# Attention of a two-layer encoder step: keys cast in parts, maxima ahead of the copies of sums, a row cleared by GpSimd

## The chip, the cores and the metric

The kernel runs on one core of a Trainium2 chip. The metric is the device time of one execution in microseconds; the median of three runs is 2562.42 us (2562.3 to 2562.77). All numbers of the trace are of one further, profiled execution.

## The reference

One inference step of two layers, over 16 learned meta tokens, a prompt of 1024 tokens and a running stream of 32 tokens with 128 past ones. Cut to what matters here:

```python
z = rmsnorm(x) @ w_in                      # query rank 768, latent 256, rotary key 32, two RG-LRU inputs of 512
q = (rmsnorm(c_q) @ w_uq)                  # 8 heads of 64 + 32 (rotary) columns
kv = ckv_keys @ w_ukv                      # per head: 64 key and 64 value columns
s = (q_nope . k_nope + q_pe . k_pe) * SM_SCALE      # rotary key k_pe is shared by all heads
s = where(key_chunk <= query_chunk, s, -1e30)
o = softmax(s) @ v
h = x + concat(rmsnorm(o), rmsnorm(y_lru)) @ w_out
h = h + square(relu(rmsnorm(h) @ w_up)) @ w_down
```

The output must hold the accuracy of float32, so the kernel splits each operand of a product into a high part (float32r) and a low part (the difference) and multiplies high by high, high by low and low by high.

## The kernel before, in words

Each engine has its own program, written out by hand; nothing schedules it but the order of the code and the waits on semaphores. `w(name, k)` waits until the semaphore `name` has come to `k` in this layer. Per layer come the input projections, the attention, the output projection, and an MLP which takes the greater part of the time. The change touches the attention alone.

The keys stand in 1296 columns (meta tokens, prompt, stream, past), the queries in 1074. Heads go in turn through two slots: even heads use `qe`, `keh`, `kel`, odd heads `qo`, `koh`, `kol` (queries, keys high, keys low). In each slot some partitions hold the head's own 64 key or query rows, others the 32 rotary rows, and one row holds the shift, which takes the maximum of each query's scores off. In the odd slot the shift row is row 32, inside the rows that the maxima's product reads (all 128), so it must be zero while maxima are made.

Before the loop over heads TensorE makes the four key products (L743, read by ScalarE into `kf`) and the ten value products (L918), with the maxima steps of head 0 among them. Then the loop goes over 8 heads and 19 pairs of a query bank and a key tile (`NP = 19`). For each pair TensorE (L946) multiplies the exponentials of three pairs ago with the values, and (L961) makes the scores of the new pair. At pairs 2 to 12 it also does one of the eleven maxima steps of the **next** head (L893, `MAXES`), on the high parts only. VectorE reduces each step from PSUM (`reduce_max`, L1986). The two PSUM banks of the maxima take turns: step s waits until the reduction of step s-2 is done. At pair 13 VectorE folds the parts together (`all_parts`, L1993), at pair 14 TensorE transposes the result (L899), ScalarE and VectorE make the shift of it (L1371, L1997), and DMAs of SyncE and GpSimd (L2502, L2503) put it into the shift row, which the next head's first scores wait for.

At the start of head h's loop VectorE loads the slot of head h+1: the rotary queries (`load_q`, L1959; for odd heads from 3 on it first clears the shift row, L1957) and the keys' high part (`load_k`, L1972). ScalarE casts the other query rows (L1350). GpSimd then makes the low parts (`low_parts`, L2476): three subtractions, two for the queries and one for the keys, after it has waited for all three high parts. The rotary keys are the same for all heads and are written once for each slot: for the odd slot VectorE casts them in the loop of head 0 (`kslot_hi`, L1976) and subtracts them to a low part at pair 4 (`kslot_lo`, L1690). The casts of head 1's keys wait for the last value product, because `koh` and `kol` lie where that product reads `ckvl`.

When a query bank is finished (pair 2, 8 or 18, seen four pairs later: at pairs 6, 12, and 3 of the next head) VectorE copies the row of sums out of PSUM (`sums_out`, L2009) and ScalarE the output. In the loops of heads 2, 4 and 6 VectorE also inverts the sums of two heads, at pair 10 (L2013).

## Time and profile before

| | |
|---|---|
| median of three runs | 2562.42 us |
| profiled execution | 2563.18 us, its span 2561.3 us |
| mean granted TensorE clock | 0.997 |
| TensorE busy | 2537.1 us (99%) |
| VectorE busy | 1767.7 us (69%) |
| ScalarE busy | 1029.1 us (40%) |
| GpSimd busy | 287.9 us (11%) |
| TensorE's share of the chain that ended last | 96% |
| of it the scores L961, values L946, maxima L893 | 4%, 5%, 2% |

PE is TensorE's matmuls, PEld its weight loads, DVE VectorE, ACT ScalarE, POOL GpSimd, SP SyncE. In a timeline a row is one instruction or several alike behind one another, with its start from the span's start, its length, and in brackets the engine's idle time in front of it and what ended that ("issue": nothing that the profile shows). Ends of matmuls are modelled, so two matmuls' lengths can overlap; their starts are the better measure. The first layer's loop over heads begins at 307 us, the second layer's at 1579 us, and a head takes some 20 us.

### The profile page before, as it was taken

The page shows a single profiled execution, that of the slowest core. Times are in us where ns is not written, and L with a number is a line of the kernel's source. Part 1 is how long each engine was busy: PE and PEld are TensorE (multiplying, and loading weights), DVE is VectorE, ACT ScalarE, POOL GpSimd, SP SyncE. Part 2 cuts the span into 40 slices and gives each one's busy share as a digit, 9 for nine tenths or more (in the row PEclk, how much of TensorE's full clock was granted, in tenths as well). Part 3 has the DMA queues.
Part 4 walks back from the last instruction along what each step waited for, and adds up shares of the span by engine and source line. Part 5 has one row for each costly group of instructions (what it writes and reads, how often), then busy time and mean ns, then how long its engine had stood idle before and what let it go on. Part 6 is the DMA issues. An engine that isn't in the chain of part 4 may idle for free.

```text
span 2561.3 us, 43462 instructions
## 1 busy us (share of the span) xinstructions
PE 2537.1 (99%) x18088; PEld 2452.9 (96%) x18088; DVE 1767.7 (69%) x2554; ACT 1029.1 (40%) x1777; POOL 287.9 (11%) x206
## 2 busy tenths in 40 slices
PE   9999999999999999999999999999999999999997
PEld 9999877999999999999999998779999999999997
DVE  8679766598666665666776796665985656666666
ACT  5464355445232322323424644553443323232325
POOL 0123344100000000000001233441000000000002
PEclk9999999999999999999999999999999999999998
DMA  4121201211121111112221121012111111121112
GB/s 157 50 65 63 59 10 40 92 57 50 34 63 38 55 46 43 58 34 67 83 81 58 58 70 51 11 45 94 50 50 50 50 42 59 34 67 34 63 38 77
DMA packets 54704, 143.86 MB, mean 56 GB/s; under 512 B 9280, under 2 KB 12448, under 8 KB 54512
## 3 DMA queue, kind: packets, MB, share of 16 engines
q1 hardware_dynamic: 49600, 129.62, 15.5%
q0 software_dynamic: 4768, 11.45, 1.4%
q8 instruction: 145, 2.38, 0.4%
q14 instruction: 47, 0.39, 0.1%
q10 hardware_dynamic: 144, 0.04, 0.0%
HBM read 127.37 MB, written 11.36 MB: 54 GB/s over the span
## 4 chain that ended last, share of the span: by engine, by line
PE 96%; DVE 2%; issue 1%; ACT 1%; DMA 1%; POOL 0%; SPq 0%; ACTq 0%; DVEq 0%; POOLq 0%
PE ps L1096 29%; PE ps L743 26%; PE ps L1067 24%; PE ps L946 5%; PE ps L961 4%; PE ps L1015 2%; PE ps L893 2%; PE ps L810 1%; PE ps L918 1%; PE ps L1093 0%; PE ps L772 0%; DMA qe<-mt 0%; PE ps L831 0%; DVE mxp L1986 0%; DVE msq L2367 0%
## 5 line engine op out<-in xcount | busy, mean ns | idle before, releaser
L2275 DVE TENSOR_TENSOR xall<-xall,ps 128x536 f32<-128x536 f32 (+1 forms) x504 | 355.6, 706 | 202.8 <-PE ps L1096 202.7
L1096 PE MATMUL ps<-fh,whi 128*128 128x268 f32 (+1 forms) x2016 | 412.4, 286 | 0.0
L1096 PE MATMUL ps<-fh,wlo 128*128 128x268 f32 (+1 forms) x2016 | 412.4, 286 | 0.0
L1096 PE MATMUL ps<-fl,whi 128*128 128x268 f32 (+1 forms) x2016 | 412.3, 286 | 0.0
L1473 ACT ACTIVATE whi<-raw 128x512 fp32r<-128x512 f32 x218 | 136.5, 628 | 561.5 <-PE ps L1096 556.4
L1096 PEld LDWEIGHTS ps<-fh,whi 128*128 128x128 f32 x2016 | 314.7, 189 | 0.3 <-issue 0.2
L1096 PEld LDWEIGHTS ps<-fl,whi 128*128 128x128 f32 x2016 | 314.1, 189 | 0.0
L1096 PEld LDWEIGHTS ps<-fh,wlo 128*128 128x128 f32 x2016 | 314.0, 189 | 0.0
L2129 DVE TENSOR_TENSOR wlo<-raw,whi 128x512 fp32r<-128x512 f32 x218 | 150.5, 692 | 195.6 <-ACT whi L1473 193.9
L1986 DVE TENSOR_REDUCE mxp<-ps 64x1 f32<-64x64 f32 (+11 forms) x384 | 140.9, 372 | 53.8 <-PE ps L893 46.9
L1145 ACT ACTIVATE whi<-raw 128x1024 fp32r<-128x1024 f32 (+3 forms) x72 | 66.7, 926 | 233.6 <-PE ps L743 231.2
L743 PE MATMUL ps<-xgh,whi 128*128 128x358 f32 (+1 forms) x720 | 157.3, 327 | 0.0
L743 PE MATMUL ps<-xgl,whi 128*128 128x358 f32 (+1 forms) x720 | 156.6, 325 | 0.0
L743 PE MATMUL ps<-xgh,wlo 128*128 128x358 f32 (+1 forms) x720 | 156.5, 325 | 0.0
L1504 ACT ACTIVATE ff<-ps 128x536 f32<-128x536 f32 (+1 forms) x96 | 59.1, 616 | 188.6 <-PE ps L1067 173.0
L743 PEld LDWEIGHTS ps<-xgl,whi 128*128 128x128 f32 x720 | 124.0, 189 | 0.0
L743 PEld LDWEIGHTS ps<-xgh,whi 128*128 128x128 f32 x720 | 123.3, 189 | 0.5 <-issue 0.2
L743 PEld LDWEIGHTS ps<-xgh,wlo 128*128 128x128 f32 x720 | 123.3, 189 | 0.0
L1662 DVE TENSOR_TENSOR wlo<-raw,whi 128x1024 fp32r<-128x1024 f32 (+3 forms) x70 | 87.3, 1247 | 40.0 <-ACT whi L1145 39.6
L1510 ACT ACTIVATE ff<-ff 128x536 f32<-128x536 f32 (+1 forms) x128 | 83.2, 650 | 76.9 <-DVE ff L2233 75.3
L2218 DVE TENSOR_TENSOR ff<-ff,ps 128x536 f32<-128x536 f32 (+1 forms) x90 | 63.8, 708 | 67.8 <-PE ps L1067 67.8
L1473 ACT ACTIVATE whi<-draw 128x512 fp32r<-128x512 f32 x128 | 80.8, 632 | 73.0 <-PE ps L1067 73.0
(556 smaller groups left out, 5836.6 us busy)
## 6 DMA issues: line engine op xcount, KB each, us to landing
raw<-in_wst SPq DMA_DIRECT2D x140, 512.0 KB, 3.7
draw<-in_wst SPq DMA_DIRECT2D x128, 256.0 KB, 2.7
xall<-in_xT SPq DMA_DIRECT2D x16, 537.0 KB, 7.4
x_scratch<-xall POOLq DMA_DIRECT2D x8, 537.0 KB, 3.4
xall<-x_scratch SPq DMA_DIRECT2D x8, 537.0 KB, 5.6
rc<-sum_scratch POOLq DMA_DIRECT2D x16, 268.0 KB, 4.1
ra<-qr SPq DMA_DIRECT2D x16, 134.2 KB, 2.4
out_ckv_out<-ckv POOLq DMA_DIRECT2D x4, 536.0 KB, 4.3
```

The source lines that it names most:

```text
L743: mm = nc.tensor.matmul(dst(q), wt, r(q), start=(k == 0 and i == 0), stop=(k == n - 1 and i == 2))
L946: mm = nc.tensor.matmul(ps[0:65, bank, c0:c0 + n], v[:, v0:v0 + 65], p_tile(gk)[:, 0:n], start=(k in FIRST), stop=(k in LAST))
L961: mm = nc.tensor.matmul(ps[:, gi % 3, 0:n], ks[e][0 if a == "h" else 1][rows, k0:k0 + P], qs[e][0 if c == "h" else 1][rows, q0:q0 + n], st ...
L1067: mm = nc.tensor.matmul(ps[:, 2 * slot_ + q, 0:HN], wt, rhs[:, q * HN:(q + 1) * HN], start=(opens and kk == 0 and i == 0), stop=(kk == 3 a ...
L1096: mm = nc.tensor.matmul(ps[:, 2 * s + q, 0:HN], wt, rhs[:, q * HN:(q + 1) * HN], start=(kk == 0 and i == 0), stop=(kk == 1 and i == 2))
L1145: nc.scalar.activation(whi[b % 2][:, 0:n], raw[b % 2][:, 0:n], ACT.Copy).then_inc(S["w_hi"], 1)
L1473: nc.scalar.activation(ring(pairs("u_hi", j) + u, whi), src, ACT.Copy).then_inc(S["u_hi"], 1)
L1510: nc.scalar.activation(ff[c][:, 0:N2], ff[c][:, 0:N2], ACT.Square).then_inc(S["f_sq"], 1)
L1662: V.tensor_tensor(wlo[b % 2][:, 0:n], raw[b % 2][:, 0:n], whi[b % 2][:, 0:n].bitcast(F32), ALU.subtract).then_inc(S["w_lo"], 1)
L1986: ins = V.reduce_max(mxp[lo_:hi_, tile, part:part + 1], ps[lo_:hi_, max_bank(h, s), c0:c0 + n], AX_X)
L2129: V.tensor_tensor(ring(spot, wlo), src, ring(spot, whi).bitcast(F32), ALU.subtract).then_inc(S["u_lo"], 1)
L2275: V.tensor_tensor(xq, xq, pair_slot(DOWN_SLOT[n % 3], L), ALU.add).then_inc(S["d_add"], 1)
```

## The change

Four edits, all in the attention.

1. **Head 1's keys in two parts.** Instead of two casts of 1296 columns (the head's keys, the rotary keys), VectorE makes both for the columns 0 to 400 and then both for the rest (`load_second`). TensorE's first three maxima steps of head 1 wait for the first parts alone, the fourth (`K_STEPS = 3`) for all.
2. **The low rotary keys in three places.** `kslot_lo` of the odd slot is cut in three pieces of 432 columns: the first right behind the casts and ahead of all reductions, the others behind the reductions at pairs 3 and 4.
3. **Maxima ahead of copies.** In each pair `reduce_max` and `all_parts` now come before `sums_out`.
4. **GpSimd clears the shift row** of heads 3, 5 and 7 (`clear_shift`), as its first step for such a head, when the scores that used the slot are done; TensorE's first maxima step of these heads waits for it. GpSimd's `low_parts` waits for the keys only ahead of its third subtraction, for every head.

```diff
+K_FIRST, K_STEPS = 400, 3
+K_PARTS = [(0, 432), (432, 864), (864, KW)]
...
@@ TensorE, max_step @@
-                        w("k_hi", h + 1)
+                        if h != 1:
+                            w("k_hi", h + 1)
...
+                        if e == 1 and h >= 3:
+                            pe.wait_ge(S["slot1_set"], L * PER["slot1_set"] + 2 + h // 2)
...
+                    if h == 1 and s == K_STEPS:
+                        w("k_hi", 2)
+                        w("kslot_hi", 3)
...
@@ VectorE @@
-                    if h % 2 == 1 and h >= 3:
-
-                        V.memset(qs[1][0][32:33, :].bitcast(F32), 0.0)
...
-                def kslot_hi(e):
-
-                    V.tensor_copy(ks[e][0][KEY_ROWS[e], :], kpe[KEY_ROWS[e], :]).then_inc(S["kslot_hi"], 1)
+
+                def load_second():
+
+                    w("mm", U_V + 10)
+                    dst, src, rows = slot_parts(1)[2]
+                    V.tensor_copy(dst[0][rows, 0:K_FIRST], src[rows, 0:K_FIRST])
+                    V.tensor_copy(ks[1][0][KEY_ROWS[1], 0:K_FIRST], kpe[KEY_ROWS[1], 0:K_FIRST]).then_inc(S["kslot_hi"], 1)
+                    V.tensor_copy(dst[0][rows, K_FIRST:KW], src[rows, K_FIRST:KW]).then_inc(S["k_hi"], 1)
+                    V.tensor_copy(ks[1][0][KEY_ROWS[1], K_FIRST:KW], kpe[KEY_ROWS[1], K_FIRST:KW]).then_inc(S["kslot_hi"], 1)
...
-                def kslot_lo(e):
-
-                    w("kslot_hi", e + 1)
-                    lo(ks[e][1][KEY_ROWS[e], :], kpe[KEY_ROWS[e], :], ks[e][0][KEY_ROWS[e], :], "kslot_lo")
+                def kslot_lo(e, a, b):
+
+                    w("kslot_hi", 3 if e else 1)
+                    lo(ks[e][1][KEY_ROWS[e], a:b], kpe[KEY_ROWS[e], a:b], ks[e][0][KEY_ROWS[e], a:b], "kslot_lo")
...
                         if i == 0 and h + 1 < NH:
                             if h:
                                 load_q(h + 1)
-                            load_k(h + 1)
-                            if h == 0:
-                                kslot_hi(1)
+                                load_k(h + 1)
+                            else:
+                                load_second()
+                                kslot_lo(1, *K_PARTS[0])
                         if h == 0 and i == 15:
                             split(30)
+                        if h + 1 < NH:
+                            if i in MX_AT:
+                                reduce_max(h + 1, MX_AT.index(i))
+                            if h == 0 and i in (3, 4):
+                                kslot_lo(1, *K_PARTS[i - 2])
+                            if i == MX_END:
+                                all_parts(h + 1)
+                                shift_lo(h + 1)
                         for n_bank in range(3):
                             hb, ib = divmod(h * NP + i - OUT_LAG - BANK_LAST[n_bank], NP)
                             if ib == 0 and hb >= 0:
                                 sums_out(hb, n_bank)
-                        if h + 1 < NH:
-                            if i in MX_AT:
-                                reduce_max(h + 1, MX_AT.index(i))
-                            if h == 0 and i == 4:
-                                kslot_lo(1)
-                            if i == MX_END:
-                                all_parts(h + 1)
-                                shift_lo(h + 1)
...
@@ GpSimd @@
+                def clear_shift(h):
+
+                    pool.wait_ge(S["s"], L * PER["s"] + (h - 1) * NP)
+                    pool.wait_ge(S["q_lo"], L * PER["q_lo"] + h)
+                    G.memset(qs[1][0][32:33, :].bitcast(F32), 0.0).then_inc(S["slot1_set"], 1)
+                    pool.wait_ge(S["slot1_set"], L * PER["slot1_set"] + 2 + h // 2)
+
                 def low_parts(h):
 
+                    if h % 2 == 1 and h >= 3:
+                        clear_shift(h)
                     w("qn_hi", h + 1)
                     w("q_hi", h + 1)
-                    w("k_hi", h + 1)
-                    for dst, src, rows in slot_parts(h):
+                    for n, (dst, src, rows) in enumerate(slot_parts(h)):
+                        if n == 2:
+                            w("k_hi", h + 1)
                         ins = G.tensor_tensor(dst[1][rows, :], src[rows, :], dst[0][rows, :].bitcast(F32), ALU.subtract)
                     ins.then_inc(S["q_lo"], 1)
```

Three places of the instruction order show what moves. The new file's lines are numbered some ten to twenty higher; a row has the line, the operation, its operands and size, and what it waits for. The first place is VectorE at the start of head 0's loop, first layer (`koh`, `kol`: the odd slot's keys; `kpe`: the rotary keys). Before:

```order
L1972 CAST koh_136<-kf0_123 64x1296 [waits mm]
L1976 CAST koh_136<-kpe_86 64x1296
L1986 TENSOR_REDUCE mxp<-ps 128x1 [waits mxmm]
L1986 TENSOR_REDUCE mxp<-ps 64x1
L1986 TENSOR_REDUCE mxp<-ps 128x1
L1986 TENSOR_REDUCE mxp<-ps 64x1
L1986 TENSOR_REDUCE mxp<-ps 16x1
L1986 TENSOR_REDUCE mxp<-ps 128x1 [waits mxmm]
L1986 TENSOR_REDUCE mxp<-ps 64x1
L1986 TENSOR_REDUCE mxp<-ps 128x1 [waits mxmm]
L1690 TENSOR_TENSOR kol_137<-kpe_86,koh_136 64x1296 [waits kslot_hi]
```

Now:

```order
L1984 CAST koh_136<-kf0_123 64x400 [waits mm]
L1985 CAST koh_136<-kpe_86 64x400
L1986 CAST koh_136<-kf0_123 64x896
L1987 CAST koh_136<-kpe_86 64x896
L1700 TENSOR_TENSOR kol_137<-kpe_86,koh_136 64x432 [waits kslot_hi]
L1997 TENSOR_REDUCE mxp<-ps 128x1 [waits mxmm]
L1997 TENSOR_REDUCE mxp<-ps 64x1
L1997 TENSOR_REDUCE mxp<-ps 128x1
L1997 TENSOR_REDUCE mxp<-ps 64x1
L1997 TENSOR_REDUCE mxp<-ps 16x1
L1997 TENSOR_REDUCE mxp<-ps 128x1 [waits mxmm]
L1997 TENSOR_REDUCE mxp<-ps 64x1
```

The low part of the rotary keys stood behind the third step's reduction; now its first third stands ahead of the first one, behind four casts, and the other two behind the second and third step's.

The second place is GpSimd's program from head 1's low parts on, first layer (`qo` and `qe` are the slots' queries, `mt` the shift). Before:

```order
L2476 TENSOR_TENSOR qo_133<-qn0_116,qo_133 64x1074 [waits k_hi,q_hi,qn_hi]
L2476 TENSOR_TENSOR qo_133<-ra0_127,qo_133 32x1074
L2476 TENSOR_TENSOR kol_137<-kf0_123,koh_136 64x1296
L2502 DMA qo_133<-mt_257 1x2x16 [waits mt_lo]
L2503 DMA qo_133<-mt_257 1x2x32
L2476 TENSOR_TENSOR qe_132<-qn1_117,qe_132 64x1074 [waits k_hi,q_hi,qn_hi]
L2476 TENSOR_TENSOR qe_132<-ra1_128,qe_132 32x1074
L2476 TENSOR_TENSOR kel_135<-kf1_124,keh_134 64x1296
L2502 DMA qe_132<-mt_257 1x2x16 [waits mt_lo]
L2503 DMA qe_132<-mt_257 1x2x32
L2476 TENSOR_TENSOR qo_133<-qn1_117,qo_133 64x1074 [waits k_hi,q_hi,qn_hi]
L2476 TENSOR_TENSOR qo_133<-ra1_128,qo_133 32x1074
```

Now:

```order
L2499 TENSOR_TENSOR qo_133<-qn0_116,qo_133 64x1074 [waits q_hi,qn_hi]
L2499 TENSOR_TENSOR qo_133<-ra0_127,qo_133 32x1074
L2499 TENSOR_TENSOR kol_137<-kf0_123,koh_136 64x1296 [waits k_hi]
L2525 DMA qo_133<-mt_257 1x2x16 [waits mt_lo]
L2526 DMA qo_133<-mt_257 1x2x32
L2499 TENSOR_TENSOR qe_132<-qn1_117,qe_132 64x1074 [waits q_hi,qn_hi]
L2499 TENSOR_TENSOR qe_132<-ra1_128,qe_132 32x1074
L2499 TENSOR_TENSOR kel_135<-kf1_124,keh_134 64x1296 [waits k_hi]
L2525 DMA qe_132<-mt_257 1x2x16 [waits mt_lo]
L2526 DMA qe_132<-mt_257 1x2x32
L2487 MEMSET qo_133 1x1074 [waits q_lo,s]
L2499 TENSOR_TENSOR qo_133<-qn1_117,qo_133 64x1074 [waits q_hi,qn_hi,slot1_set]
```

The wait `k_hi` has moved from the first to the third subtraction of every head, and one memset stands ahead of head 3's.

The third place is VectorE at pairs 10 to 14 of head 1's loop, first layer (`srow`: the row of sums; `mx`: the folded maxima). Before:

```order
L1986 TENSOR_REDUCE mxp<-ps 128x1 [waits mxmm] x3
L1986 TENSOR_REDUCE mxp<-ps 64x1 x2
L1986 TENSOR_REDUCE mxp<-ps 128x1 [waits mxmm]
L2009 COPY srow_147<-ps 1x384 [waits pv]
L1986 TENSOR_REDUCE mxp<-ps 128x1 [waits mxmm]
L1986 TENSOR_REDUCE mxp<-ps 64x1
L1993 TENSOR_REDUCE mx<-mxp 128x10 [waits mxt,mxred]
```

Now:

```order
L1997 TENSOR_REDUCE mxp<-ps 128x1 [waits mxmm] x3
L1997 TENSOR_REDUCE mxp<-ps 64x1 x2
L1997 TENSOR_REDUCE mxp<-ps 128x1 [waits mxmm] x2
L1997 TENSOR_REDUCE mxp<-ps 64x1
L2020 COPY srow_147<-ps 1x384 [waits pv]
L2004 TENSOR_REDUCE mx<-mxp 128x10 [waits mxt,mxred]
```

The copy of the sums has moved from ahead of the eleventh step's two reductions to behind them, directly ahead of the folding reduction.

## Rows read from the trace of the kernel before

**Rows 1.** Timeline of TensorE, loop of head 0 (columns: start, length, engine, line, operands)
```profile
309.34 0.48 PE L893 MATMUL ps<-koh,qo 128*128 128x144 f32 x3 [0.94 <-DVE koh L1976]
...
311.95 0.34 PE L893 MATMUL ps<-koh,qo 128*128 128x400 f32 x1
...
315.94 0.51 PE L893 MATMUL ps<-koh,qo 128*128 128x144 f32 x2 [0.53 <-DVE mxp L1986]
...
1587.51 0.50 PE L893 MATMUL ps<-koh,qo 128*128 128x144 f32 x2 [0.52 <-DVE mxp L1986]
```

**Rows 2.** Timeline of VectorE, loops of heads 0 and 1, first layer
```profile
307.18 0.83 DVE L1972 CAST koh<-kf 64x1296 fp32r<-64x1296 f32 x1 [3.09 <-PE ps L918]
...
308.04 0.83 DVE L1976 CAST koh<-kpe 64x1296 fp32r<-64x1296 f32 x1
...
309.86 2.08 DVE L1986 TENSOR_REDUCE mxp<-ps 128x1 f32<-128x80 f32 x7 [0.99 <-PE ps L893]
...
312.83 2.32 DVE L1690 TENSOR_TENSOR kol<-kpe,koh 64x1296 fp32r<-64x1296 f32 x1
...
330.22 1.28 DVE L1986 TENSOR_REDUCE mxp<-ps 128x1 f32<-128x80 f32 x5 [1.27 <-PE ps L893]
```

**Rows 3.** Timeline of GpSimd, loop of head 0, first layer
```profile
304.06 0.51 POOL L2503 DMA_DIRECT2D qe<-mt  x1
...
308.18 3.04 POOL L2476 TENSOR_TENSOR qo<-qn,qo 64x1074 fp32r<-64x1074 f32 x1 [3.61 <-DVE koh L1972]
...
313.84 4.11 POOL L2476 TENSOR_TENSOR kol<-kf,koh 64x1296 fp32r<-64x1296 f32 x1
```

**Rows 4.** Timelines of GpSimd and VectorE where the rotary keys are made
```profile
209.28 3.11 POOL L2436 TENSOR_TENSOR sqa<-sqa,sqa 128x1074 f32<-128x1074 f32 x1 [1.27 <-ACT sqa L1277]
...
210.47 2.49 DVE L1865 COPY kpe<-kpe 32x1074 f32<-32x1074 f32 x1
```

**Rows 5.** Timelines of VectorE and TensorE, opening of head 2's loop
```profile
347.00 0.95 DVE L1957 MEMSET qo<- 1x1074 f32 x1 [2.69 <-PE ps L961]
...
347.97 0.71 DVE L1959 CAST qo<-ra 32x1074 fp32r<-32x1074 f32 x1
...
349.75 0.49 PE L893 MATMUL ps<-koh,qo 128*128 128x144 f32 x3 [0.30 <-issue]
```

**Rows 6.** Timelines around the keys of head 0 (last row: second layer)
```profile
281.48 0.83 DVE L1972 CAST keh<-kf 64x1296 fp32r<-64x1296 f32 x1 [0.69 <-ACT kf L1362]
...
282.48 2.50 POOL L2476 TENSOR_TENSOR qe<-qn,qe 64x1074 fp32r<-64x1074 f32 x1 [1.28 <-DVE keh L1972]
...
283.20 0.70 PE L893 MATMUL ps<-keh,qe 96*128 96x144 f32 x4
...
1553.88 2.49 POOL L2476 TENSOR_TENSOR qe<-qn,qe 64x1074 fp32r<-64x1074 f32 x1 [0.85 <-DVE keh L1972]
```

**Rows 7.** Timelines of TensorE and VectorE, pairs 12 to 14 of head 1's loop
```profile
341.37 0.41 PE L893 MATMUL ps<-keh,qe 96*128 96x512 f32 x1
...
341.44 0.56 DVE L2009 COPY srow<-ps 1x384 f32<-1x384 f32 x1
...
342.93 0.20 DVE L1993 TENSOR_REDUCE mx<-mxp 128x10 f32<-128x40 f32 x1
...
343.21 0.29 PE L899 MATMUL ps<-ident,mx 128*128 128x128 f32 x1
```

**Rows 8.** The same place in head 2's loop
```profile
361.29 0.69 DVE L1986 TENSOR_REDUCE mxp<-ps 128x1 f32<-128x512 f32 x1
...
361.44 0.42 PE L893 MATMUL ps<-koh,qo 128*128 128x512 f32 x1
```

**Rows 9.** GpSimd clearing rows, L2493 (min/median/max ns, first and last start)
```profile
L2493 POOL MEMSET qo<- x4: 987/988/989, 291.1 to 1563.5; 32x1074 f32 x4
```

**Rows 10.** TensorE's waits; windows: us, busy of the engines, granted clock, DMA share
```profile
PE ps L997 <- POOL msq L2542: 4.8, 1, 4.8
...
2550.00:2555.00 5.00, 2.04 (x4) 1.17 (x4) 3.73 (x10) 2.17 (x3) 0.00 (x0) 0.50 0.93 339
```

More of the change, by code:

```diff
@@ L472, in trunk @@
             ("y_sq", 4), ("y_sum", 3), ("y_n", 4), ("v_one", 1), ("v_ev", 10), ("kf", 4),
-            ("kslot_hi", 2), ("kslot_lo", 2),
-            ("slot1_set", 2), ("p_zero", 5), ("qn_hi", NH), ("q_hi", NH), ("k_hi", NH), ("q_lo", NH), ("s", NH * NP), ("p", NH * NP),
+            ("kslot_hi", 3), ("kslot_lo", 4),
+            ("slot1_set", 2 + NH // 2 - 1), ("p_zero", 5), ("qn_hi", NH), ("q_hi", NH), ("k_hi", NH), ("q_lo", NH), ("s", NH * NP), ("p", NH * NP),
             ("pv", NH * NP), ("mxmm", NH * NMX), ("mxred", NH * NMX), ("mxc", NH), ("mxt", NH), ("mt_hi", NH), ("mt_lo", NH),
@@ L956, in _ @@
                             if h == 1:
-                                w("kslot_lo", 2)
+                                w("kslot_lo", 4)
                         if gi >= 3:
@@ L1964, in load_k @@
                         w("kf", 1)
-                    if h == 1:
-                        w("mm", U_V + 10)
                     if h == 2:
@@ L2005, in sums_out @@
                     if h == 0 and n == 0:
-                        w("kslot_lo", 2)
+                        w("kslot_lo", 4)
                     r = slice(64 * (h % 2), 64 * (h % 2) + 1)
@@ L2031, in _ @@
                     if s == 3:
-                        kslot_lo(0)
+                        kslot_lo(0, 0, KW)
                     if s == 7:
```

## The prediction

> **What bounds the kernel now.** I read the waits of TensorE first. In this stage they are short, and a stage in which TensorE hardly waits can gain only what those waits are. Then I read the first head of the attention loop, engine by engine, since the change rewrites its opening. Here s0 to s10 are the eleven steps that compute a head's maxima (L893), r0 to r10 VectorE's reductions of them (L1986), and "head 1" is the second head, whose maxima are made while head 0's scores run.
>
> TensorE waits at s0 of head 1 for the rotary half of the keys, 0.94 us, and at s5 for r3, 0.53 us [rows 1]. VectorE explains both. It casts the two halves of the keys (0.83 us each), then reduces, and subtracts the low rotary part (L1690) in one piece of 2.32 us in front of r3 [rows 2]. That piece ought to be shorter: GpSimd was at work beside it [rows 3]. So the third view is GpSimd's, and the question is what happens when both read SBUF.
>
> The trace answers it. A GpSimd operation ran from 209.28 to 212.39; a VectorE copy of 32x1074, started at 210.47, took 2.49 us, where the cast of that shape takes 0.71 [rows 4, 5]. It ended 0.57 us behind GpSimd's end: it had stood still. It goes the other way too: GpSimd's qo operation at 308.18 took 3.04 us against 2.50 for its like [rows 3, 6], since the cast begun at 308.04 held it up. And they take turns: VectorE's 2.32 us subtraction began at 312.83, was held until GpSimd's operation ended (just before 313.84) and needed 1.37 more; GpSimd's next one, from 313.84, then took 4.11 us. **One waits for the whole instruction of the other.**
>
> The Trainium skill says the same more widely (SBUF — State Buffer, "SBUF: two separate sides"): the port pair of VectorE and GpSimd is an exclusive lock, and a VectorE operation in a 2-port mode or with two SBUF inputs, and a GpSimd operation, block each other for an instruction's length. The trace agrees for the 2.49 us copy; that a cast is held up in the same way no row here shows alone. By this rule the change is slower, and the rule is my forecast's mechanism; without it the sum would be the second rival's.
>
> **The change part by part.**
>
> *GpSimd no longer waits for the keys before a head's two query subtractions.* For head 1 both queries are ready long before, so they start behind the shift DMAs, at 304.06 + 0.51 = 304.57 [rows 3], 3.6 us earlier than now. At 2.50 us each [rows 6] they hold GpSimd until about 307.15 and 309.7 (at 2.1 us each, a bound from 3.04 less the cast's part of it, until 308.9). VectorE's first key cast starts at 307.18 [rows 2]: it falls into the second one, or slips in and its successor waits. Call the moment at which GpSimd's second operation ends U; I take 309.5 (308.9 to 309.9).
>
> *The keys of head 1 in two parts.* From 0.83 us at 1296 columns and 0.71 at 1074 [rows 2, 5] a column costs 0.54 ns and an instruction 0.13 us: 0.35 us for 400 columns, 0.61 for 896. The first cast, held up, ends 0.2 behind U, the second at U + 0.58. TensorE started s0 0.47 us after the last cast's end now (308.04 + 0.83 to 309.34), so s0 comes at U + 1.05 = 310.55, against 309.34: 1.2 us late, where a free port would have made it 0.9 early.
>
> *The rest of the keys and the first third of the low part, ahead of r0.* The two 896-column casts end at U + 1.22 and U + 1.86. The first of them releases GpSimd's kol operation, which asks while the second runs, and is next: about 2.8 us (4.11 less the 1.3 that it was held up) until U + 4.7. The low piece of 432 columns asks in the meantime and waits; it ends at U + 5.15 (a third of 1.37). Only then r0, 1.28 us (the five pieces at 330.22), until U + 6.46 = 315.95. s2 needs r0: it starts at 316.0 against 311.95. TensorE would have come to it at 310.55 + 2.61 = 313.15, so it waits 2.85 us in one piece. From s2 to s5 TensorE needs 3.99 us with the wait of 0.53 in it [rows 1], 3.46 without; the two later thirds (0.5 us each, GpSimd done) fit between r1, r2 and r3. s5 comes at 319.45 against 315.94: **3.5 us per layer, 7.0 in both**; the second layer has the same wait at s5 (1587.51). With U from 308.9 to 309.9 it is 2.9 to 3.9 per layer.
>
> *The same in head 0.* GpSimd was free from 282.48 - 1.28 = 281.20 and stood for the keys' cast [rows 6]. Now it starts at once, and the cast, ready at 281.48, waits until 281.26 + 2.50 = 283.76 and ends at 284.45. TensorE's s0, at 283.20 now with no wait, comes at about 284.55: 1.3 us (0.9 to 1.5). In the second layer the cast ended at about 1553.88 - 0.17 = 1553.71 (GpSimd followed it by 0.17 in the first: 281.48 + 0.83 = 282.31 to 282.48), so it had begun at about 1552.85, before GpSimd came free (1553.88 - 0.85 = 1553.03): it keeps the port, and this costs nothing.
>
> *Maxima ahead of copies of sums.* At pairs 3 and 6 VectorE swaps two operations that it runs back to back; nobody waits for either. At pair 12 the copy moves from in front of r10 to behind it, in front of the reduction (L1993) that the transpose waits for. VectorE ends r9 just before 341.44, TensorE s10 only at 341.37 + 0.41 = 341.78 [rows 7]. Now the copy fills that pause. After the change VectorE stands until 341.82 and does r10 and the copy, which take 342.93 - 341.44 = 1.49 us together: L1993 starts at 343.31, 0.38 later. The transpose (343.21) follows L1993's end (343.13) within 0.08 and would wait 0.30 to 0.38; I take 0.35. In heads 2, 4 and 6 the reciprocal has pushed r9 to 361.29, s10 ends at 361.86 before r9 does, and the order is free [rows 8]. Left are the loops of heads 0, 1, 3 and 5 in two layers: 8 x 0.35 = **2.8 us**. The DMAs behind the transpose move with TensorE, and give nothing back.
>
> *GpSimd clears the odd heads' shift row.* VectorE's memset of 0.95 us goes (347.00), and TensorE waits 0.30 us at s0 there (349.75) [rows 5, 9]. GpSimd's memset takes 0.99 for 32 rows of that width; the trace shows none of one row, and I take the same. It asks when VectorE casts the query: cast 0.71, memset, then the key cast of 0.83, ends at about 349.35 against 349.54 now. If the port is not shared for a memset, the gain is all of 0.30; if GpSimd is late, it is nothing. I take 0.2 in five of six places: -1.0 (0 to -1.8). The new wait in front of s0 is met by 348.7. Behind it GpSimd's query subtractions wait, which are needed some 15 us later.
>
> **Sum:** 7.0 + 1.3 + 2.8 - 1.0 = +10.1 us on the profiled execution's 2563.18, so 2573.3; that execution lies 0.76 over the median of 2562.42, which gives **2572.5**.
>
> **The rivals.**
> - *Only the casts are held up.* If the low piece gets the port before GpSimd's kol operation, r0 starts at U + 2.4, s2 at 313.25, s5 at 316.7: 0.8 per layer. Sum 1.6 + 1.3 + 2.8 - 1.0 = 4.7, so 2567.1. For it: the order in which two waiting engines are served is seen in few places. Against it: GpSimd asks first.
> - *No cast is held up (not slower).* Then s0 comes 0.9 us earlier (the wait of 0.94 is gone), r0 is done by 311.1 when s2 wants it, and s5 comes at 308.44 + 2.61 + 3.46 = 314.5: -1.4 per layer at most. With -1.5 from the odd heads (five times 0.30) and +2.8 from the transposes the sum is -1.5, so 2560.9; if the transposes do not wait either, 2558.1, still within 0.2%. It decides for this side once the cast at 307.18 takes under 0.4 us. Against it speaks the 2.49 us copy.
> - *The clock falls too.* TensorE stands 2.85 us at s2, shortly after some 2 us at s0. A wait of 4.8 us near the end of the kernel was followed by a stretch at a granted clock of 0.50, the 1.2 GHz level [rows 10]. If each layer's stall is followed by 4 us at that level, work of 2 us is lost each time: 4 more, 2576.5.
>
> **How the numbers follow.** The forecast has 0.62 (its own range 2569 to 2576), only the casts 0.14, no blocking 0.12, the clock 0.12. The range of 2564 to 2578 leaves out most of the second rival and the worst of the third. A difference of 0.2% (5.1 us) is about what a measurement tells from no change. Slower by more takes the forecast, the clock and a small part of the first rival: 0.78; same 0.17, faster 0.05.
>
> **What would show it.** Right: VectorE's first 400-column cast, or the one behind it, takes 1.5 to 2.5 us; GpSimd's kol operation directly behind the last cast; a low piece of about 3.3 us in front of r0; TensorE's longest wait in the stage, near 3 us, at the third maxima step of head 1, for r0; eight waits of 0.3 to 0.4 at the transposes of heads 0, 1, 3 and 5's loops, where there were none. Wrong: casts of 0.35 us with GpSimd busy beside them, or a loop of head 0 that is no longer than before.

## The result, and the profile after

The changed kernel is slower, as forecast: 2571.25 us (2570.23 to 2572.82, 7 runs) against 2562.64 us (2562.3 to 2563.45, 7 runs), ratio 1.0034 with a 95% interval of 1.0023 to 1.0044. The forecast was 2572.5, range 2564 to 2578. In the profiled executions the span grew from 2561.3 to 2569.4 us, 8.1 us.

Two of TensorE's waits at the maxima steps (engine, line waited for: us in total, times, longest) have grown. The kernel before waited there 1.5 us in five short waits (0.3 at the longest) and 0.9 for the rotary keys' cast, against the first row; and 1.0 us in two waits for reductions, against the second row. Of the 4.4 us, 1.3 are head 0's, at its first maxima step:

```profile
PE ps L903 <- issue: 4.4, 3, 2.0
...
PE ps L903 <- DVE mxp L1997: 3.8, 2, 2.7
```

One kind is gone: the kernel before had this, six waits of the transposes of the maxima in the loops of heads 2, 4 and 6, and no row for them is left.

```profile
PE ps L899 <- DVE mx L1993: 1.8, 6, 0.3
```

VectorE's timeline, first layer: head 0's keys, and the opening of head 0's loop, to set beside [rows 2, 6]:

```profile
281.63 2.98 DVE L1977 CAST keh<-kf 64x1296 fp32r<-64x1296 f32 x1 [0.70 <-ACT kf L1372]
...
308.87 0.37 DVE L1984 CAST koh<-kf 64x400 fp32r<-64x400 f32 x1 [3.09 <-PE ps L928]
...
309.25 2.55 DVE L1985 CAST koh<-kpe 64x400 fp32r<-64x400 f32 x1
...
311.83 0.62 DVE L1986 CAST koh<-kf 64x896 fp32r<-64x896 f32 x1
...
312.49 0.62 DVE L1987 CAST koh<-kpe 64x896 fp32r<-64x896 f32 x1
...
313.14 3.23 DVE L1700 TENSOR_TENSOR kol<-kpe,koh 64x432 fp32r<-64x432 f32 x1
...
316.29 1.93 DVE L1997 TENSOR_REDUCE mxp<-ps 128x1 f32<-128x80 f32 x7
```

GpSimd's timeline of the same stretch, beside [rows 3, 6]:

```profile
281.42 2.50 POOL L2499 TENSOR_TENSOR qe<-qn,qe 64x1074 fp32r<-64x1074 f32 x1
...
306.33 2.53 POOL L2499 TENSOR_TENSOR qo<-qn,qo 64x1074 fp32r<-64x1074 f32 x1
...
308.92 2.66 POOL L2499 TENSOR_TENSOR qo<-ra,qo 32x1074 fp32r<-32x1074 f32 x1
...
312.53 3.37 POOL L2499 TENSOR_TENSOR kol<-kf,koh 64x1296 fp32r<-64x1296 f32 x1 [0.96 <-DVE koh L1986]
```

The keys' cast of head 0 takes 2.98 us in place of 0.83. It is ready at 281.63, GpSimd's subtraction runs until 283.92, and 0.69 later the cast is done. In the loop GpSimd's second query subtraction (308.92) starts 0.05 us behind VectorE's first cast; that cast runs freely, and its successor, from 309.25, waits for the end of GpSimd's at 311.58 and then takes 0.22 us. The next two casts take 0.62 each. GpSimd's key subtraction (312.53) is held until the last cast ends at 313.11, and the low piece of 432 columns (313.14) takes 3.23 us, of which it stands 2.8 behind GpSimd. Only then comes the first reduction.

TensorE's first maxima steps of head 1 (first layer, then second) and its granted clock, the second fence with the columns us of the stretch, busy time of PE, PEld, DVE, ACT and POOL, granted clock, DMA share and GB/s:

```profile
312.15 0.48 PE L903 MATMUL ps<-koh,qo 128*128 128x144 f32 x3 [2.00 <-issue]
...
317.62 0.45 PE L903 MATMUL ps<-koh,qo 128*128 128x400 f32 x1 [1.10 <-DVE mxp L1997]
...
321.01 0.45 PE L903 MATMUL ps<-koh,qo 128*128 128x144 f32 x2
...
1586.98 0.49 PE L903 MATMUL ps<-koh,qo 128*128 128x144 f32 x3 [1.10 <-issue]
...
1592.50 0.50 PE L903 MATMUL ps<-koh,qo 128*128 128x400 f32 x1 [2.74 <-DVE mxp L1997]
...
1597.50 0.45 PE L903 MATMUL ps<-koh,qo 128*128 128x144 f32 x2
```

```profile
308.50:312.00 3.50, 1.64 (x11) 1.24 (x9) 3.08 (x3) 1.71 (x9) 3.02 (x2) 1.00 0.06 22
...
312.00:314.00 2.00, 1.85 (x7) 1.50 (x8) 1.94 (x3) 0.00 (x0) 1.47 (x1) 0.69 0.00 0
...
314.00:316.00 2.00, 2.00 (x7) 1.61 (x7) 2.00 (x1) 0.58 (x3) 1.90 (x1) 0.50 0.00 0
...
316.00:318.00 2.00, 0.90 (x5) 0.52 (x4) 1.93 (x8) 0.49 (x1) 0.00 (x0) 0.95 0.00 0
...
1592.00:1594.00 2.00, 1.50 (x8) 1.45 (x8) 1.90 (x7) 0.00 (x0) 0.00 (x0) 0.69 0.00 0
...
1594.00:1596.00 2.00, 2.00 (x7) 1.29 (x6) 1.55 (x5) 0.47 (x3) 0.00 (x0) 0.50 0.00 0
```

s5 starts at 321.01, 5.07 us later than in [rows 1]; the loop had begun 1.74 us later. The last fence shows what the forecast had only as a rival: a stretch at a granted clock of 0.50, the 1.2 GHz level, in each layer. In the first layer it comes behind the wait of 2.0 us at s0 and lasts about 3.4 us (from the shares of the windows 312 to 318). It lies in front of s2, which has to wait for r0 anyway; since TensorE works slowly there, only 1.10 us of that wait are left. In the second layer the waits are 1.10 us at s0 and 2.74 at s2, and the low stretch begins behind s2 and is paid in full: from s2 to s5 TensorE takes 5.00 us there (1592.50 to 1597.50) against 3.39 in the first.

The opening of head 2's loop, beside [rows 5], and VectorE at pairs 12 and 13 of head 1's, beside [rows 7]:

```profile
352.23 1.58 DVE L1966 CAST qo<-ra 32x1074 fp32r<-32x1074 f32 x1 [2.63 <-PE ps L971]
...
352.25 0.99 POOL L2487 MEMSET qo<- 1x1074 f32 x1 [1.08 <-PE ps L971]
```

```profile
347.04 0.86 DVE L1997 TENSOR_REDUCE mxp<-ps 128x1 f32<-128x464 f32 x2 [0.41 <-PE ps L903]
...
347.82 0.55 DVE L2020 COPY srow<-ps 1x384 f32<-1x384 f32 x1
...
348.40 0.20 DVE L2004 TENSOR_REDUCE mx<-mxp 128x10 f32<-128x40 f32 x1
...
348.65 0.33 PE L909 MATMUL ps<-ident,mx 128*128 128x128 f32 x1
```

GpSimd's memset and VectorE's cast start together, and the cast takes 1.58 us: 0.71 and most of the memset's 0.99. The folding reduction starts 1.36 us behind the start of r10 (347.04 to 348.40), not 1.49, and the transpose is 0.22 us late, the matmul behind it 0.26.

Counted by the start of the same matmuls in both traces, the 8.0 us are: head 0's keys +1.6 (first layer alone; 0.15 of it was there before the keys); the loops of head 0 to s5 +3.3 and +4.8; all the rest about -1.8. In this rest the transposes' eight delays of 0.23 stand against six gains of 0.25, and the odd heads' openings and the waits for shift DMAs gain some 0.8 us in the first layer and 1.7 in the second. Outside the loops over heads the distance moves by +0.5 us between the layers and -0.5 at the end; no run here shows why.

### The profile page after: what moved, and what is told of

Same layout as the page of the kernel before. It is cut to its first block, busy times and chain, and to the rows that moved or that the text cites. A ratio compares the mean times of both kernels' runs of the same rounds, so it can differ in the third digit from the quotient of the medians.

```text
span 2569.4 us, 43480 instructions
## 1 busy us (share of the span) xinstructions
PE 2542.2 (99%) x18088; PEld 2455.4 (96%) x18088; DVE 1774.2 (69%) x2556; ACT 1029.1 (40%) x1777; POOL 296.4 (12%) x212
## 3 DMA queue, kind: packets, MB, share of 16 engines
q1 hardware_dynamic: 49600, 129.62, 15.4%
## 4 chain that ended last, share of the span: by engine, by line
PE 96%; DVE 2%; issue 1%; DMA 0%; ACT 0%; POOL 0%; SPq 0%; DVEq 0%; ACTq 0%; POOLq 0%
PE ps L1106 29%; PE ps L747 27%; PE ps L1077 24%; PE ps L956 5%; PE ps L971 4%; PE ps L1025 2%; PE ps L903 2%; PE ps L928 1%; PE ps L814 1%; PE ps L835 1%; DVE mxp L1997 0%; PE ps L1103 0%; PE ps L776 0%; DVE srow L2020 0%; DVE msq L2379 0%
```

## The experiments

All were timed against the kernel before, which ran at 2563.1 to 2563.5 us in these groups; shifts are of the same matmul's start in two traces.

| | kernel | median us | ratio to before, 95% interval |
|---|---|---|---|
| 1 | before, queries alone | 2572.18 | 1.0035 (1.0021 to 1.0048) |
| 2 | the same, wait filled | 2567.66 | 1.0018 (1.0009 to 1.0027) |
| 3 | changed kernel, GpSimd waits for keys first | 2569.97 | 1.0026 (1.0015 to 1.0036) |
| 4 | changed kernel, port free at the opening | 2558.92 | 0.9982 (0.9973 to 0.9991) |
| 5 | changed kernel, low piece behind r0 | 2567.55 | 1.0017 (1.0008 to 1.0026) |
| 6 | before, head 0's queries alone | 2564.87 | 1.0006 (0.9997 to 1.0015) |
| 7 | before, copies alone | 2563.68 | 1.0001 (0.9992 to 1.0010) |
| 8 | before, clearing alone | 2562.21 | 0.9996 (0.9987 to 1.0005) |
| 9 | port free, copy behind the fold | 2555.81 | 0.9971 (0.9960 to 0.9982) |
| 10 | the same, keys in one part | 2557.45 | 0.9975 (0.9966 to 0.9984) |

**1. The queries' early start alone.** On the kernel before:

```diff
                     w("q_hi", h + 1)
-                    w("k_hi", h + 1)
-                    for dst, src, rows in slot_parts(h):
+                    for n, (dst, src, rows) in enumerate(slot_parts(h)):
+                        if n == 2:
+                            w("k_hi", h + 1)
```

> The kernel before with one part of the change alone: GpSimd's query subtractions no longer wait for the keys. Theory 'port': head 0's keys' cast 2.98 us in the first layer (+1.6 us), the second cast of head 1's keys held until GpSimd's second query subtraction ends (2.5 us instead of 0.83), the first maxima step of head 1 1.7 us later in each layer, of which the low rotary part, no longer held up (1.4 us instead of 2.3), gives 0.5 to 0.9 back: 2566 us (2564.5 to 2568). Theory 'order': no cost, since GpSimd only ends earlier: 2562.6 us.

VectorE's second cast and TensorE's first maxima step in its trace:

```profile
309.44 2.98 DVE L1976 CAST koh<-kpe 64x1296 fp32r<-64x1296 f32 x1
...
312.88 0.79 PE L893 MATMUL ps<-koh,qo 128*128 128x144 f32 x3 [3.09 <-DVE koh L1976]
```

The cast takes 2.98 us in place of 0.83, and TensorE waits 3.09 us for it. That is the port. But the kernel came out at 2572.18, slower than the 2566 expected and no faster than the whole change: moving this one wait is enough for all of its loss. The shift at s0 is 3.54 us in the first layer and grows to 6.2 behind it, in which no engine waits for another more than before. The windows show why (columns as above):

```profile
310.00:312.00 2.00, 0.00 (x0) 0.00 (x0) 2.00 (x1) 0.36 (x3) 1.94 (x2) 0.93 0.00 0
...
312.00:314.00 2.00, 1.12 (x4) 0.94 (x5) 0.69 (x3) 0.00 (x0) 2.00 (x1) 0.50 0.00 0
...
316.00:318.00 2.00, 2.00 (x7) 1.71 (x6) 0.73 (x2) 0.46 (x3) 0.00 (x0) 0.50 0.00 0
```

**2. Is it the clock?** The same kernel, with work put where TensorE stood:

```diff
+                    if s == 0 and h == 1:
+                        w("v_ev", 10)
+                        for _ in range(12):
+                            nc.tensor.matmul(ps[:, 4, 0:512], qs[0][0][0:96, NMETA:NMETA + P], ks[0][0][0:96, 0:512],
+                                             start=True, stop=True, skip_group_check=True)
```

> The kernel with GpSimd's query subtractions alone moved (e4_queries_only, 2572.2 us), in which TensorE waits 3.1 us for head 1's keys and then runs for some 6 us at half clock; here twelve further matmuls of 512 columns (2.8 us, result not used) stand in front of that wait. Theory 'clock': TensorE does not idle, the granted clock stays at 1.00, the next matmuls run at full pace, and 2.5 us in the first and 2.8 in the second layer come back: 2567 us. Rival, the slow stretch is the port's or PSUM's doing and not the clock's: it stays as it is, 2572 us or more.

The twelve matmuls per layer write a PSUM bank that nothing reads before it is written anew. A window of this kernel (columns as above), and below it the second cast and s0 in its timeline:

```profile
314.00:316.00 2.00, 2.00 (x14) 1.80 (x13) 1.52 (x6) 0.98 (x4) 1.13 (x1) 1.00 0.00 0
```

```profile
309.29 3.02 DVE L1981 CAST koh<-kpe 64x1296 fp32r<-64x1296 f32 x1
...
312.78 0.48 PE L898 MATMUL ps<-koh,qo 128*128 128x144 f32 x3 [0.17 <-issue]
```

The second cast is held up as before (3.02 us) and s0 starts as late, yet the clock stays at 1.00 and the kernel is 4.5 us faster with 24 matmuls more. Without them the trace has a stretch of about 6.8 us at 0.50 in each layer. So of the 8.8 us of experiment 1 about half is the waits, half the clock behind them.

**3. The keys' wait back in front.** On the changed kernel:

```diff
-                    for n, (dst, src, rows) in enumerate(slot_parts(h)):
-                        if n == 2:
-                            w("k_hi", h + 1)
+                    w("k_hi", h + 1)
+                    for dst, src, rows in slot_parts(h):
```

> The changed kernel with one part undone: GpSimd waits for a head's keys ahead of all three subtractions again. Theory 'port' (VectorE and GpSimd block each other for a whole instruction): the keys' cast of head 0 takes 0.83 us again instead of 2.98, and the four casts of head 1's keys 0.37, 0.37, 0.62, 0.62 us, so the first maxima step of head 1 comes 1.2 us behind the first cast's start instead of 3.3; but GpSimd's first query subtraction of head 1 now starts beside the casts and holds up the first low piece (about 2.5 us instead of 3.2), and the third maxima step still waits some 2 us. The loop of head 0 about 2.5 us shorter than in the changed kernel in each layer, head 0's keys 1.6 us earlier in the first: 2564.5 us (2563 to 2566). Theory 'order' (the cost is the low piece and the longer list of casts ahead of the first reduction, GpSimd's early start does no harm): only head 0's 1.6 us come back, 2569.5 us, and the casts of head 1 are as long as before.

A miss: 2569.97. The number is that of the theory 'order', 2569.5, but its mechanism is not what the trace shows: by it the casts would have stayed long, and they are short (0.36 us for 400 columns), as the port theory said. s0 came 1.1 us earlier than before the change; but the low pieces, now three, met GpSimd's three subtractions (timeline of VectorE and TensorE):

```profile
309.23 2.78 DVE L1700 TENSOR_TENSOR kol<-kpe,koh 64x432 fp32r<-64x432 f32 x1
...
313.26 0.45 PE L903 MATMUL ps<-koh,qo 128*128 128x400 f32 x1 [2.25 <-DVE mxp L1997]
...
315.33 2.74 DVE L1700 TENSOR_TENSOR kol<-kpe,koh 64x432 fp32r<-64x432 f32 x1
...
318.86 0.81 PE L903 MATMUL ps<-koh,qo 128*128 128x144 f32 x2 [1.96 <-DVE mxp L1997]
```

The first and third piece take 2.78 and 2.74 us where a free one takes 0.60 (experiment 4), so TensorE waits at s2 and again 1.96 us at s5. I had counted one collision. The wait at s5 goes with the lower clock (0.50 in the stretch 320 to 322 of this trace); the longer one at s2 is not (1.00 from 312 to 318). Cut in pieces and set between GpSimd's operations, the low part waits two to three times; in the kernel before it waited once, and TensorE waited 0.53 us at s5 for the reduction behind it [rows 1, 2].

**4. The port kept free.** On the changed kernel, GpSimd's program alone: head 0 waits for its keys first; head 1's query subtractions stand ahead of the shift DMAs of head 0; its key subtraction waits for the last low piece. VectorE's order is untouched.

```diff
+                    if h == 0:
+                        w("k_hi", 1)
...
+                        if n == 2:
+                            w("k_hi", h + 1)
+                            if h == 1:
+                                w("kslot_lo", 4)
...
+                low(1, (0, 1))
                 few_shifts(0)
                 for h in range(1, NH):
-                    low_parts(h)
+                    if h == 1:
+                        low(1, (2,))
+                    else:
+                        low_parts(h)
```

> The changed kernel, but GpSimd works only when VectorE does not need the shared port at this place: head 0 waits for its keys first, head 1's two query subtractions come ahead of the shift DMAs of head 0, and its key subtraction behind all three low pieces of VectorE. VectorE's order, with the low piece ahead of the first reduction, is untouched. Theory 'port': casts 0.37, 0.37, 0.62, 0.62 us, low pieces 0.5 to 0.6 each, third maxima step without a wait, no stretch at half clock; the loop of head 0 is 1 to 1.4 us shorter than in the kernel before, the rest as in the changed kernel: 2559 us (2557.5 to 2560.5), faster than before. Theory 'order': the loop of head 0 stays 2 us or more longer than before, 2567 us or more.

VectorE's timeline, the second cast and the first low piece:

```profile
307.50 0.36 DVE L1985 CAST koh<-kpe 64x400 fp32r<-64x400 f32 x1
...
309.20 0.60 DVE L1700 TENSOR_TENSOR kol<-kpe,koh 64x432 fp32r<-64x432 f32 x1
```

As expected, 2558.92: 12.3 us faster than the changed kernel by GpSimd's order alone, and 0.18% faster than the kernel before. The low piece stands ahead of the first reduction here too, and costs nothing. TensorE waits at none of the maxima steps of head 1, and the clock stays at 1.00 from 308 to 328 us and at the same place of the second layer.

**5. The low piece behind r0.** On the changed kernel:

```diff
                                 load_second()
-                                kslot_lo(1, *K_PARTS[0])
...
-                            if h == 0 and i in (3, 4):
+                            if h == 0 and i in (2, 3, 4):
```

> The changed kernel with the first low piece behind the first reduction instead of in front of it. Theory 'port': the casts of head 1 are held up as before (one of them 2.5 us); GpSimd's key subtraction then holds up the low piece for some 1.5 us, but the first reduction, which reads PSUM and one SBUF port less, runs free beside it: the third step's wait falls from 3 us to under 1, a later one at the fourth step takes part of it back. As in the other kernels with such a wait at the first step, TensorE runs some 4 to 6 us at half clock behind it, and now that work stands in the open: together 0.5 to 1 us per layer gained, 2570 us (2569 to 2571). Theory 'order' (the low piece in front of the reduction is the loss): 2.9 us per layer come back, 2565.5 us.

The timeline, s0, the first low piece and s2:

```profile
311.85 0.79 PE L903 MATMUL ps<-koh,qo 128*128 128x144 f32 x3 [1.91 <-issue]
...
313.96 2.13 DVE L1700 TENSOR_TENSOR kol<-kpe,koh 64x432 fp32r<-64x432 f32 x1
...
316.08 0.34 PE L903 MATMUL ps<-koh,qo 128*128 128x400 f32 x1
```

2567.55: outside the 2569 to 2571 expected, a miss, and between the two theories' numbers. r0 runs beside GpSimd unhindered, the piece is held up for 1.5 us of its 2.13, and s2 waits for nothing. The loop of head 0 to s5 costs 2.0 us in the first layer and 3.4 in the second, against 3.3 and 4.8: 2.7 us less. I had taken too much for the clock in the open: its stretch here is about 3.4 us long in the first layer and costs 1.6 us up to s2, and in the second about 6.8 us, for 2.9:

```profile
1588.00:1590.00 2.00, 2.00 (x8) 1.60 (x7) 2.00 (x2) 0.58 (x3) 1.17 (x1) 0.50 0.05 8
...
1590.00:1592.00 2.00, 2.00 (x11) 1.90 (x11) 1.92 (x5) 0.54 (x2) 0.00 (x0) 0.54 0.00 0
```

But the whole wait at s2 had been longer still. This profiled execution took 2569.17 us, 1.6 over the median, at a mean granted clock of 0.995. One other of the eleven is like it (2569.01, 0.995); the rest lie at 2567.1 to 2568.5 with 0.996 to 0.998. So the low stretches can differ between executions of one kernel; that the second layer's is the shorter one in the faster executions fits these numbers, but no trace shows it.

**6. Head 0 alone.** On the kernel before, the wait moved for head 0 only:

```diff
-                    w("k_hi", h + 1)
-                    for dst, src, rows in slot_parts(h):
+                    if h:
+                        w("k_hi", h + 1)
+                    for n, (dst, src, rows) in enumerate(slot_parts(h)):
+                        if n == 2 and h == 0:
+                            w("k_hi", 1)
```

> The kernel before with one thing alone: for head 0 GpSimd's query subtractions no longer wait for the keys. Theory 'port': in the first layer the keys' cast takes 2.9 us instead of 0.83 and all that follows comes 1.3 to 1.6 us later; in the second layer the cast has the port first and nothing moves: 2563.9 to 2564.2 us. Rival: the later keys are caught up in the four key products: 2562.6 us.

VectorE's cast of head 0's keys, first layer and second:

```profile
281.44 2.98 DVE L1972 CAST keh<-kf 64x1296 fp32r<-64x1296 f32 x1 [0.70 <-ACT kf L1362]
```

```profile
1554.17 0.83 DVE L1972 CAST keh<-kf 64x1296 fp32r<-64x1296 f32 x1 [0.42 <-ACT kf L1362]
```

The cast takes 2.98 us in the first layer and 0.83 in the second, where it had begun 0.06 us before GpSimd asked. The time, 2564.87, is 1.7 us over before, 0.7 more than expected at most, and by its interval no proof by itself; the shift of 1.4 us at TensorE's first maxima step is.

**7. The copies alone.** On the kernel before:

```diff
-                        for n_bank in range(3):
...
-                                sums_out(hb, n_bank)
                         if h + 1 < NH:
...
                                 shift_lo(h + 1)
+                        for n_bank in range(3):
...
+                                sums_out(hb, n_bank)
```

> The kernel before with the maxima ahead of the copies of sums alone. Prediction on record: a wait of 0.35 us at eight transposes, none given back, 2565.4 us. From the changed kernel's trace: 0.23 us at each of the eight (heads 0, 1, 3 and 5's loops), but 0.25 us gained in each of the six others that waited before (loops of heads 2, 4, 6), together +0.3 us: 2562.9 us, not to be told from before.

No difference in time. In its trace the transposes of the loops of heads 0, 1, 3 and 5 come 0.21 to 0.23 us later each, those of heads 2, 4 and 6 0.23 to 0.25 earlier. The same operations in another order take VectorE less: from the start of the first of copy and r10 to the fold's it was 1.49 us in [rows 7]; here it is 1.36 (VectorE's timeline, head 1's loop):

```profile
341.98 0.86 DVE L1986 TENSOR_REDUCE mxp<-ps 128x1 f32<-128x464 f32 x2 [0.41 <-PE ps L893]
...
343.34 0.20 DVE L1993 TENSOR_REDUCE mx<-mxp 128x10 f32<-128x40 f32 x1
```

**8. The clearing alone.** On the kernel before, with TensorE's wait for it:

```diff
-                    if h % 2 == 1 and h >= 3:
-
-                        V.memset(qs[1][0][32:33, :].bitcast(F32), 0.0)
...
+                    if h % 2 == 1 and h >= 3:
+                        clear_shift(h)
```

> The kernel before with GpSimd clearing the shift row of heads 3, 5 and 7, and nothing else. Theory 'port': the memset (0.99 us) and VectorE's first cast start together, one is held up, and the keys' cast ends only 0.1 to 0.3 us earlier than before: TensorE's first maxima step of these heads 0.2 to 0.5 us earlier, four to six times, together -1.5 us (0 to -2): 2561 us. Theory 'no port for a memset': VectorE's cast takes 0.71 us as ever and 0.95 us are free in front of each of six, but TensorE can take only what it waited, 0.5 us in four to six places: -2.5 us. The cast's length tells them apart.

VectorE and GpSimd at the opening of head 2's loop:

```profile
346.63 1.58 DVE L1958 CAST qo<-ra 32x1074 fp32r<-32x1074 f32 x1 [2.44 <-PE ps L963]
...
346.65 0.99 POOL L2473 MEMSET qo<- 1x1074 f32 x1 [1.15 <-PE ps L963]
```

The cast takes 1.58 us, so a memset takes the port too. TensorE's waits of 0.3 us at s0, four in the kernel before (in front of heads 3 and 7, both layers), are gone all the same. The time, 2562.21, is 0.9 us under before and not to be told from it.

**9. The copy behind the fold.** On the kernel of experiment 4:

```diff
                             if i == MX_END:
                                 all_parts(h + 1)
+                                sums_out(h, 1)
                                 shift_lo(h + 1)
...
-                            if ib == 0 and hb >= 0:
+                            if ib == 0 and hb >= 0 and (n_bank != 1 or h + 1 == NH):
```

> The version with the port free at head 1's opening (e2_ports_free, 2558.9 us) with the third copy of sums behind the folding reduction instead of in front of it, ahead of a wait that VectorE has there anyway. The transposes then no longer wait: 0.23 us in eight places and 0.2 in six: 2556 us (2555 to 2557.5), faster than before and than the changed kernel.

2555.81, as expected: the fastest version, 0.29% faster than before and 15.4 us faster than the changed kernel. VectorE copies in a pause it had anyway (fold, copy, and TensorE's transpose):

```profile
341.43 0.20 DVE L2004 TENSOR_REDUCE mx<-mxp 128x10 f32<-128x40 f32 x1
...
341.66 0.56 DVE L2020 COPY srow<-ps 1x384 f32<-1x384 f32 x1
...
341.93 0.27 PE L909 MATMUL ps<-ident,mx 128*128 128x128 f32 x1
```

**10. The keys in one part.** On the kernel of experiment 9:

```diff
                             else:
-                                load_second()
+                                load_k(1)
+                                V.tensor_copy(ks[1][0][KEY_ROWS[1], :], kpe[KEY_ROWS[1], :]).then_inc(S["kslot_hi"], 1)
                                 kslot_lo(1, *K_PARTS[0])
```

The waits for these casts follow: TensorE's s0 of head 1 waits for both whole casts.

> The fastest version so far (b1_best, 2555.8 us) with head 1's keys cast in one part each again, as in the kernel before; the rest as it is. It sizes the cast in two parts where the port is free. The first maxima step of head 1 waits for 2 x 0.86 us of casts instead of 2 x 0.38: 0.9 us later in the first layer, 0.4 to 0.9 in the second, of which nothing is given back: 2557.4 us (2557 to 2557.8). Rival: TensorE's later start is caught up at the fifth or sixth step, where VectorE's reductions set the pace: 2556 us.

2557.45, as expected: with the port free the cast in two parts is worth 1.6 us, or 1.3 when each is set against the kernel before of its own group (2563.13 and 2563.49). The intervals in the table overlap; the single times do not (2555.2 to 2556.0 against 2556.9 to 2558.1).

## Why the prediction was right, point by point

- **One engine waits for the whole instruction of the other: shown** (experiments 1, 4, 6). Head 0's cast, by the forecast's times 2.97 us, took 2.98; head 1's second cast, forecast at 1.5 to 2.5, took 2.55, the low piece 3.23 for "about 3.3", and all of this is gone when only GpSimd's order changes. The Trainium skill's rule (SBUF — State Buffer, "SBUF: two separate sides") holds here for VectorE's casts and its subtraction of two SBUF inputs beside GpSimd's subtractions (for two inputs the page limits the rule to GpSimd operations that read SBUF, as these do), and for a cast beside GpSimd's memset. The page also says that whichever starts first has the ports for its whole instruction; the cast at 352.23 started 0.02 us ahead of the memset by the profile and was held up.
- **Head 1's opening: right in the first layer, short of the clock in the second.** U (the end of GpSimd's second query subtraction) was 311.6, which is 2.7 us behind the first cast's start for 2.3 forecast (2.7 at its latest). s5 came 3.3 us later than the loop's start in the first layer; forecast 3.5. The wait of 2.85 us at s2 "in one piece" came only in the second layer (2.74); in the first it was 1.10, because TensorE came to s2 late at the lower clock, and r0 alone set when s2 began. In the second layer s5 came 4.8 later: the added 1.3 to 1.6 are the clock, which stood in the forecast as a rival. Its size in the forecast, 4 us more in all, was too much for the changed kernel, since in the first layer the slow stretch is hidden by the wait for r0.
- **Head 0's keys: right**, 1.6 us (1.5 from the keys themselves) for 1.3 (0.9 to 1.5), and nothing in the second layer.
- **The transposes: wrong in size.** Forecast +2.8 us; measured eight delays of 0.23 and six gains of 0.25, +0.3 us. The step that failed is "the order is free" in heads 2, 4 and 6, and the taking of 1.49 us for the pair. The six transposes of these heads already waited 0.3 us each in the kernel before (1.8 in all), so any time that VectorE saves there shows; the forecast overlooked that row. And the pair is shorter in the new order, 1.36 us: VectorE lets an operation begin before the one ahead is through (r10 of 0.86 us starts at 347.04, the copy at 347.82), and the two reductions behind one another followed by the copy are quicker than before.
- **The odd heads: right** within its bounds, though its working is not: 0.71, 0.99 and 0.83 us from 347.00 end at 349.53, not at 349.35, so that by its own terms nothing was gained. In the trace cast and memset met as forecast, and the key cast ends 2.44 us behind the opening of VectorE's work in place of 2.53; the opening itself comes sooner behind TensorE's last score. Alone it gave 0.9 us (experiment 8), not told from none. From the loop of head 1 on, all but the transposes' share gives about 2 us in the changed kernel, some of it from shorter waits for shift DMAs, which were not in the forecast.
- **That the number came within 1.25 us is in part luck: errors cancel.** Between the profiled executions the forecast was too high by 2.5 us (transposes), 0.2 (loop of head 0, first layer) and some 0.9 (odd heads, waits for shift DMAs and the rest), and too low by 1.3 (clock) and 0.3 (head 0's keys), 2.0 in all. It then took off 0.76, by which the kernel before's profiled execution lay over its median; the changed kernel's lay on it.

What the change was worth without its collision is measured by experiment 4: -4.5 us. What stays open is how the two engines' turn is settled when both ask within 0.05 us: the cast at 308.87 went ahead of the subtraction that started 0.05 us behind it, but the cast at 352.23 stood for the memset that started 0.02 us behind it.

## What to carry to other kernels

Letting an engine start earlier is free only if the ports, not just the data, are free: look up what the neighbour does in exactly that stretch, and put GpSimd's long two-input operations where VectorE reads PSUM. A short instruction cut out of a long one may wait longer than the whole did; three pieces can meet three operations. A TensorE wait of 2 to 3 us can cost another 1.6 to 2.3 us behind it (second layer of the changed kernel; experiment 2, per layer).

## What the runs showed of the hardware

- The granted clock was 0.50 during or behind waits of 1.9 to 3.1 us at s0, s2 or s5, for about 3.4 or 6.8 us, while TensorE worked again. Not every wait did it: one of 2.25 us (experiment 3, s2) did not. In the second layer waits of 0.70 and 1.25 us shortly behind one another did (experiment 5), where 0.83 and 1.10 in the changed kernel did not. With the wait filled by matmuls it stayed at 1.00.
- A VectorE reduction from PSUM ran at its usual length (1.27 us) beside GpSimd's subtraction (experiment 5), where a subtraction with two inputs in SBUF stood still.
- A GpSimd memset of one row takes as long as one of 32 rows (0.99 us) and held up a VectorE cast by 0.87 us.
